# A hybrid diffusion layer on one core: the mLSTM's gate rows are multiplied third, and three merge-gate tiles move to other stages

## The reference

```python
p = split_in(h @ w_in)      # h: modulated RMSNorm of x; pc likewise for the context
y_a = mlstm_branch(q, k, v, o, gates)     # bidirectional, chunkwise
y_b = mla_branch(...)                     # latent attention
y_c = natten_branch(...)                  # neighbourhood attention
g_a, g_b, g_c = jnp.split(jax.nn.sigmoid(gate_pre), 3, axis=-1)   # the merge gates
y = (g_a * y_a + g_b * y_b + g_c * y_c) @ w_out
x = x + g1 * y
x = x + g2 * sqrelu_mlp(rms_norm(x, g_norm2) * (1 + sc2) + sh2, w_ff1, w_ff2)
```

## Time and profile before

| | us |
|---|---|
| median of 3 runs | 1851.31 (1850.52 to 1851.66) |
| the profiled execution: its time | 1852.28 |
| its span | 1850.6 |
| PE busy | 1663.7 |
| DVE, ACT, POOL busy | 972.6, 781.6, 668.1 |

### The profile page before, as it was taken

How to read it: one execution, slowest core, us unless ns; L and a number is a source line. 1 busy time by engine, 2 the same in 40 slices (tenths; PEclk the granted TensorE clock), 3 DMA queues, 4 the chain that set the end, 5 groups by cost and what they waited for, 6 DMA issues and landing times.

```text
span 1850.6 us, 24651 instructions
## 1 busy us (share of the span) xinstructions
PE 1663.7 (90%) x9536; PEld 1397.9 (76%) x9536; DVE 972.6 (53%) x1751; ACT 781.6 (42%) x1484; POOL 668.1 (36%) x389
## 2 busy tenths in 40 slices
PE   6998989899878988899999998978999788689998
PEld 3876779767666667688888886977977676589998
DVE  5855817662334545349496964143244264546665
ACT  4334734343645432432323234347434564245443
POOL 0632434412233001445454553524633342124443
PEclk9998999999989999999999999989999898889999
DMA  8432443401214113224354743322421232335553
GB/s 334 187 135 103 156 134 146 148 23 36 86 53 137 29 55 133 92 93 177 140 182 168 281 165 114 100 85 89 149 69 51 90 106 68 141 115 173 185 184 120
DMA packets 68059, 232.72 MB, mean 126 GB/s; under 512 B 18280, under 2 KB 22760, under 8 KB 54376
## 3 DMA queue, kind: packets, MB, share of 16 engines
q1 hardware_dynamic: 60880, 213.67, 32.9%
q10 hardware_dynamic: 7064, 17.49, 2.5%
...
## 4 chain that ended last, share of the span: by engine, by line
PE 70%; DVE 10%; ACT 10%; issue 4%; POOL 3%; DMA 2%; DVEq 0%; SPq 0%; ACTq 0%
PE bank L1683 33%; PE bank L1765 8%; PE bank L1721 7%; PE bank L1703 4%; PE bank L2033 4%; PE bank L2012 3%; PE bank L1747 2%; PE bank L2019 2%; ACT wH L770 2%; POOL wL L657 1%; DMA raw<-in_p_out 1%; DVE acc L1164 1%; PE bank L1914 1%; DVE mjunk L1161 1%; POOL wL L659 1%
## 5 line engine op out<-in xcount | busy, mean ns | idle before, releaser
L657 POOL TENSOR_TENSOR wL<-raw,wH 128x1280 fp32r<-128x1280 f32 (+4 forms) x146 | 307.4, 2105 | 610.7 <-ACT wH L770 610.7
L770 ACT ACTIVATE wH<-raw 128x768 fp32r<-128x768 f32 (+7 forms) x396 | 296.7, 806 | 538.5 <-PE bank L1683 353.2
L659 POOL TENSOR_TENSOR wL<-raw,wH 128x768 fp32r<-128x768 f32 (+3 forms) x198 | 322.3, 1628 | 392.9 <-ACT wH L770 392.8
L1683 PE MATMUL bank<-hH,wH 128*128 128x512 f32 (+1 forms) x704 | 241.7, 343 | 4.6 <-DVE oL L1556 2.9
L1683 PE MATMUL bank<-hL,wH 128*128 128x512 f32 (+1 forms) x704 | 239.6, 340 | 0.0
L1683 PE MATMUL bank<-hH,wL 128*128 128x512 f32 (+1 forms) x704 | 239.6, 340 | 0.0
L1683 PE MATMUL bank<-oH,wH 128*128 128x512 f32 (+1 forms) x576 | 196.8, 342 | 5.0 <-DVE wL L1146 5.0
L1683 PE MATMUL bank<-oL,wH 128*128 128x512 f32 (+1 forms) x576 | 195.6, 340 | 0.0
L1683 PE MATMUL bank<-oH,wL 128*128 128x512 f32 (+1 forms) x576 | 195.6, 340 | 0.0
L1164 DVE SCALAR_TENSOR_TENSOR acc<-acc,cb 128x1024 f32<-128x1024 f32 x88 | 170.9, 1955 | 2.5
L1721 PE MATMUL bank<-hH,wH 128*128 128x512 f32 (+1 forms) x384 | 141.6, 369 | 25.7 <-ACT gst L798 12.2
...
## 6 DMA issues: line engine op xcount, KB each, us to landing
raw<-in_p_ff SPq DMA_DIRECT2D x64, 1024.0 KB, 4.8
acc<-in_p_mod SPq DMA_DIRECT2D x44, 1024.0 KB, 5.6
raw<-in_p_ml SPq DMA_DIRECT2D x12, 1024.0 KB, 5.9
raw<-in_p_na SPq DMA_DIRECT2D x12, 1024.0 KB, 5.6
...
raw<-in_p_out SPq DMA_DIRECT2D x8, 1024.0 KB, 6.9
```

The source lines that it names most:

```text
L657: pool.tensor_tensor(l_[:, 0:cut], r_[:, 0:cut], h_[:, 0:cut].bitcast(F32), ALU.subtract)
L659: pool.tensor_tensor(l_[:, cut:k * w], r_[:, cut:k * w], h_[:, cut:k * w].bitcast(F32), ALU.subtract)\
L770: act.activation(flat(wH, n)[:, part], flat(raw, n)[:, part], ACT.Copy)\
L1683: ins = pe.matmul(dst, w_[:, kk, c:c + P], r_[:, kk, lo:TOK], start=kk == k0 and m == 0, stop=kk == k0 + kn - 1 and m == 2)
```

## The change

The gate-row block becomes key ("ml", l, 2), behind q and k; the values are 3 and 4, the output gate 5 and 6. On PE the small transposes stand between the two halves of block 3 and behind it, the transposes to columns (now to bank 5) between blocks 5 and 6. DVE does its part of the gate rows between the values' copies, and `mod(5)` to `mod(7)` move behind parts of it. ACT's exp and ln move up behind block 3. The part "chain" is gone: "last" has 4 tiles in place of 3, "cn" 5 and 6 in place of 3 and 4. `TURN` becomes branch 0, then 2, then 1. SP's modulation loads move to other places between the weight loads. Layer 0's tile 19 is loaded ahead of the key-value block. The blocks of two kinds, "wo" and "ff", may only be placed at multiples of their size.

Cut: renumbered lists in `gate_range`, `gate_bank` and `gates`, where the name "chain" goes.

```diff
--- before.py
+++ after.py
@@ -144,13 +144,13 @@
 MOD_START, MOD_PROJ, MOD_LOOP, MOD_ML = 4, 8, 14, 20
-LOOP_MODS = (3, 4, 8, 9, 10, 11, 12, 13)
+LOOP_MODS = (1, 2, 5, 6, 7, 8, 9, 10)
...
 GATES = 24
-TURN = [(2, c) for c in range(6)] + [(0, c) for c in range(KC)] + [(2, 6), (2, 7)] + [(1, c) for c in range(KC)]
-FILL = (dict(chain=3, loop=8, last=3, cn=3, units=(0, 2, 0, 1, 1, 1, 1, 1)),
-        dict(chain=3, loop=8, last=3, cn=4, units=(1, 1, 1, 1, 1, 1)))
+TURN = [(branch, c) for branch in (0, 2, 1) for c in range(KC)]
+FILL = (dict(loop=8, last=4, cn=5, units=(0, 2, 0, 1, 1, 1, 1, 1)),
+        dict(loop=8, last=4, cn=6, units=(1, 1, 1, 1, 1, 1)))
@@ -200,13 +200,11 @@
         both(("dq", l, 0), ("dq", l, 1), ("dk", l, 0), *(g[T] for T in gate_range(l, "cn")))
-        at = gate_range(l, 0).start
-        if l == 0:
-            load += [("uq", l, 0), g[at], g[at + 1], ("uq", l, 1), ("ukv", l, 0), *g[at + 2:]]
-            use += [("uq", l, 0), g[at], g[at + 1], ("uq", l, 1), *g[at + 2:at + 6], ("ukv", l, 0), *g[at + 6:]]
-        else:
-            load += [("uq", l, 0), g[at], ("uq", l, 1), g[at + 1], ("ukv", l, 0), *g[at + 2:]]
-            use += [("uq", l, 0), g[at], ("uq", l, 1), *g[at + 1:at + 5], ("ukv", l, 0), *g[at + 5:]]
+        stages = [("uq", l, k // 2 if l == 0 else k) for k in range(4 if l == 0 else 2)] + [("ukv", l, 0)] * 4
+        for k, key in enumerate(stages):
+            fill = [g[T] for T in gate_range(l, k)]
+            load += ([key] if stages.index(key) == k else []) + fill
+            use += ([key] if key not in stages[k + 1:] else []) + fill
         both(*(("ms", l, c) for c in range(KC)), *(("to", l, j) for j in range(4)),
@@ -429,7 +427,7 @@
             if name == "ml":
-                return (packed("p_ml", l, j), KC, BLK) if j < 6 else (packed("p_gk", l, 0), KC, 64)
+                return (packed("p_gk", l, 0), KC, 64) if j == 2 else (packed("p_ml", l, j - (j > 2)), KC, BLK)
             if name == "ff":
@@ -446,7 +444,7 @@
                 return max(RANK[m] if m >= 0 else -1 for m in held[at:at + size])
-            at_ = min(range(QUARTERS - size + 1), key=lambda at: (last_use(at), at))
+            at_ = min(range(0, QUARTERS - size + 1, size if KEYS[n][0] in ("wo", "ff") else 1), key=lambda at: (last_use(at), at))
             place.append(at_ * QUARTER)
@@ -589,8 +585,8 @@
                 load("ml", 0, j)
-                if MOD_START + j - 2 < MOD_PROJ:
-                    load_mod(MOD_START + j - 2)
+                if j != 5:
+                    load_mod(MOD_START + j - 2 - (j == 6))
             for l in range(DEPTH):
@@ -861,24 +857,24 @@
                 u0 = U0["ml", l]
+                tag = f"ml{l}_"
                 act.wait_ge(*S("spilled").at(16 * (l + 1)))
...
                             act.activation(m_k[:, b, :], full(u0 + j, b)[:, :], ACT.Copy).then_inc(free(u0 + j, b), 1)
-                        if j in (4, 5):
-                            act.activation(m_o[:, 2 * (j - 4) + b, t0:], full(u0 + j, b)[:, t0:TOK], ACT.Sigmoid)\
+                        if j in (5, 6):
+                            act.activation(m_o[:, 2 * (j - 5) + b, t0:], full(u0 + j, b)[:, t0:TOK], ACT.Sigmoid)\
                                 .then_inc(free(u0 + j, b), 1)
-                tag = f"ml{l}_"
-
-                exp_and_ln()
-                for d in range(2):
-                    act.wait_ge(*S(tag + "nz").at(d + 1))
-                    link(act.activation(m_e[d][0:4, :], m_e[d][0:4, :], ACT.Exp))
-                for d in range(2):
-                    act.activation(m_e[d][0:4, :], m_e[d][0:4, :], ACT.Ln, bias=1.0).then_inc(S(tag + "ln").up(1), 1)
-                gates_out(l, "chain")
+                    if j == 3:
+                        exp_and_ln()
+                        for d in range(2):
+                            act.wait_ge(*S(tag + "nz").at(d + 1))
+                            link(act.activation(m_e[d][0:4, :], m_e[d][0:4, :], ACT.Exp))
+                        for d in range(2):
+                            act.activation(m_e[d][0:4, :], m_e[d][0:4, :], ACT.Ln, bias=1.0)\
+                                .then_inc(S(tag + "ln").up(1), 1)
@@ -1247,26 +1243,28 @@
                     mod(MOD_START)
-                    mod(MOD_START + 1)
-                for j in (2, 3):
-                    for b in range(2):
-                        free(dve.tensor_copy(m_v[:, 2 * b:2 * b + 2, 2 * j - 4:2 * j - 2, 0:ML_DV],
-                                             full(u0 + j, b)[:, :].rearrange("p (t h w) -> p t h w", t=2, h=2)), u0 + j, b)
-                    if l == 0:
-                        mod(MOD_START + j)
+
+                def values_out(j, b):
+
+                    free(dve.tensor_copy(m_v[:, 2 * b:2 * b + 2, 2 * j - 6:2 * j - 4, 0:ML_DV],
+                                         full(u0 + j, b)[:, :].rearrange("p (t h w) -> p t h w", t=2, h=2)), u0 + j, b)
...
                 narrow = m_tmp[0:64, :]
-                free(dve.tensor_copy(narrow, full(u0 + 6, 0)[0:64, :]), u0 + 6, 0)
-                freed(u0 + 6, 0)
-                free(dve.tensor_tensor(narrow, narrow, full(u0 + 6, 1)[0:64, :], ALU.add), u0 + 6, 1)
+                free(dve.tensor_copy(narrow, full(u0 + 2, 0)[0:64, :]), u0 + 2, 0)
+                freed(u0 + 2, 0)
+                free(dve.tensor_tensor(narrow, narrow, full(u0 + 2, 1)[0:64, :], ALU.add), u0 + 2, 1)
                 dve.wait_ge(*S(tag + "turned").at(1))
...
                     .then_inc(S(tag + "small").up(1), 1)
+                values_out(3, 0)
                 for d in range(2):
...
                     dve.scalar_tensor_tensor(e, z, -1.0, z, ALU.mult, ALU.min).then_inc(S(tag + "nz").up(1), 1)
+                values_out(3, 1)
+                if l == 0:
+                    mod(MOD_START + 1)
                 for d in range(2):
@@ -1291,8 +1289,13 @@
                     dve.wait_ge(*S(tag + "nmrow").at(k))
+                for b in range(2):
+                    values_out(4, b)
+                if l == 0:
+                    mod(MOD_START + 2)
+                    mod(MOD_START + 3)
                 dve.wait_ge(*S(tag + "gT").at(1))
-                dve.tensor_copy(stat[:, 128:192], bank[3][:, 0:64]).then_inc(S(tag + "gcol").up(1), 1)
+                dve.tensor_copy(stat[:, 128:192], bank[5][:, 0:64]).then_inc(S(tag + "gcol").up(1), 1)
                 k = S(tag + "gcol").n
@@ -1753,11 +1756,13 @@
-            def tokens(n, u, k, parts, sH, sL, at=None):
+            def tokens(n, u, k, parts, sH, sL, at=None, only=None):
...
                 for b, part in enumerate(parts):
+                    if only not in (None, b):
+                        continue
                     bk = begin(u, b)
@@ -1832,35 +1837,35 @@
                 first_units(n0, u0, both(KC, t0), both(KC, 0), hH, hL, lambda kk: low_ready(l, 0, kk))
-                tokens(n0 + 2, u0 + 2, KC, two, hH, hL)
-                tokens(n0 + 3, u0 + 3, KC, two, hH, hL)
-                features(n0 + 4, u0 + 4, KC, both(KC, t0), hH, hL)
-                features(n0 + 5, u0 + 5, KC, both(KC, t0), hH, hL)
-                H, L = weights(n0 + 6)
+                H, L = weights(n0 + 2)
                 for b in range(2):
-                    dst = begin(u0 + 6, b)[0:64, :]
+                    dst = begin(u0 + 2, b)[0:64, :]
                     for kk in range(4 * b, 4 * b + 4):
...
                                             start=kk == 4 * b and m == 0, stop=kk == 4 * b + 3 and m == 2)
-                    filled(ins, u0 + 6, b)
-                drained(u0 + 7)
+                    filled(ins, u0 + 2, b)
+                tokens(n0 + 3, u0 + 3, KC, two, hH, hL, only=0)
+                pe.wait_ge(*S(f"bank_free{2 * (u0 % 2) + 1}").at((u0 + 2) // 2 + 1))
                 for t in range(NTILE):
...
                 ins.then_inc(S(tag + "turned").up(1), 1)
+                tokens(n0 + 3, u0 + 3, KC, two, hH, hL, only=1)
                 pe.wait_ge(*S(tag + "small").at(1))
...
                     ins.then_inc(S(tag + "rows").up(1), 1)
-                gates(l, "chain")
+                tokens(n0 + 4, u0 + 4, KC, two, hH, hL)
+                features(n0 + 5, u0 + 5, KC, both(KC, t0), hH, hL)
                 for d in range(2):
...
                         at = (d * 4 + t) * 4
-                        pe.transpose(bank[3][:, at:at + 4], m_g[0:4, d, t * P:t * P + P], ident[0:4, 0:4])
-                        ins = pe.transpose(bank[3][:, 32 + at:36 + at], m_rows[0:4, 2 + d, t * P:t * P + P], ident[0:4, 0:4])
+                        pe.transpose(bank[5][:, at:at + 4], m_g[0:4, d, t * P:t * P + P], ident[0:4, 0:4])
+                        ins = pe.transpose(bank[5][:, 32 + at:36 + at], m_rows[0:4, 2 + d, t * P:t * P + P], ident[0:4, 0:4])
                 ins.then_inc(S(tag + "gT").up(1), 1)
+                features(n0 + 6, u0 + 6, KC, both(KC, t0), hH, hL)
                 pe.wait_ge(*S(tag + "gcol").at(1))
@@ -1891,7 +1896,7 @@
```

(4 more changed lines are left out.)

6 lines of the change are left out of this document (2 added, 4 removed).

## The result

The changed kernel takes 1868.82 us (median of 4 runs, 1868.0 to 1871.56). The ratio of its runs to those of the kernel before, estimated with its 95% interval, is 1.0103 (1.0085 to 1.012). The prediction was no change at 1851.5 us, with a range from 1843 to 1859: the change is slower, by 17.5 us against the 1851.31 of before. The profiled execution took 1868.0 us, its span is 1866.3 us, 15.7 more than before.

A forecast was written before the change was run, and what follows sets the result against it. PE, busy nine tenths of the span, bounds the kernel; time is won only where it idles or runs at half clock. Terms +1.2 - 1.2 + 0.4 - 1.1 + 0.9 = +0.2 us on 1852.3, so median 1851.5; range 1843 to 1859.

The forecast's parts named there:

- Part 9: Layer 0's weight loads: tile 3 lands just in time, from 38 us for DVE's list and 43.5 for PE.
- tile 3's weights come late: Slower rival, layer 0: modulations 5 to 7 lengthen beside POOL, delaying tile 3's load; 4 to 5 us lost, chance 0.16.
- Part 5: Loop's second broadcast: PE idle for ACT's chain, 4.5 us in layer 0, 2.5 in layer 1, plus clock 2.0 and 1.0.
- Part 3: Before block 4: PE waits for its split, 5.2 us in layer 0, 4.4 in layer 1, plus clock 2.0 and 1.5.
- Part 8: Inside the loop: small waits for tile splits go, but ACT's chain starts at the same place; 0, bound -1.5 us.
- Part 2: Before block 3: PE waits for its split, which the gate-row block mostly covers; 0.8 us left in each layer.
- Part 1: Three moved tiles in "last" and "cn": same price, waits of 5.7 and 3.2 us not filled; 0, bounds 0 and -8.
- Part 7: ACT elsewhere: +0.4 us at layer 0's first square, -1.1 in its second query stage, +0.9 in layer 1's "last".
- Part 4: Gate chain: blocks 4 and 5 hide DVE's rows, so 4.1 us go; the wait for a gate tile's low half goes too.

The follow-up runs named there:

- e_load: The changed kernel with SP's modulation loads 8 and 9 moved behind tiles 3 and 4, so tile 3 loads ahead of them: 1857.31 us.
- e_clock: The changed kernel with 22 extra products of 128x512, result unused, in PE's wait before block 4, both layers: 1861.63 us.
- e_tiles: The kernel before with only the move of the three gate tiles to "last" and "cn", the gate rows staying last: 1885.88 us.
- e_ring: The changed kernel with an 18th quarter in the ring, the gate-row block at the ring's end, and `mjunk` in bfloat16: 1851.71 us.

## Why the prediction was wrong

**Part 9, tile 3's DMA, is the step that failed first.** It said "just in time", with 5.5 us to spare, from 38 us for DVE and 43.5 for PE. PE's 43.5 was 44.2; DVE's 38 was 44.8. Term by term, predicted and measured: to the first results 4.6 and 7.8, modulation 5 at 10 and 9.0, the rows 10 and 13.1, the copies 1.4 and 1.2, modulations 6 and 7 at 12 and 13.8. So 6.3 of the 6.8 us lie in the gate rows' own operations, which were put at their price of before, when POOL was idle beside them. In the changed kernel they ran while POOL split: 3.19 us for an operation of 0.68, and 3.25 for a scan of 0.74. The prediction had the outcome as its rival "tile 3's weights come late", at 4 to 5 us, with a chance of 0.16. Measured is 9.24 - 4.5 = 4.7 against the forecast and 9.24 - 3.60 = 5.6 against e_load, which shows the cause. The path was the right one (SP's order, ACT at tile 3's split, the exponential behind it); what made DVE late was not: the rival had it from the modulation instructions, and these together took 0.7 us more than predicted. That its price came out right is in part luck.

**Part 5, the second broadcast's wait.** Layer 0, without tile 3: 4.5 predicted, 3.60 in e_load. Layer 1: 2.5 predicted, 4.57 measured. ACT's chain behind PE's end took the predicted time (6.8, measured 1225.45 to 1232.19). PE's work in it was put at 4.3 us from the kernel before, but those broadcasts and scores had run at 1.2 GHz; at 2.4 they take 2.3. The same slip made the old stretch look better than it was: its clock loss was counted for 2.3 us behind the wait and not for the 5.3 us of broadcasts and scores ahead of it, which take about 2.7 at 2.4 GHz. So of the 4.9 us by which this term and layer 1's clock were short, about 2.6 cancel. That the stretch came out at +0.9 for -1.2, and not further off, is luck.

**Parts 3 and 5, the clock.** The four falls were placed right. They were put at 2.0, 1.5, 2.0 and 1.0 us, in all 6.5, and each cost 2.4 to 3.0, in all 10.7, whether the wait ahead was 4.6 or 9.2 us long. e_clock shows the pair at block 4 as 2.6 and 2.4 us.

**Part 8 and the rest of the kernel.** "0" for stages that the change doesn't touch left out that the clock falls elsewhere when all is moved in time: +1.6 in layer 0's loop, about +3.3 in "cn", about +1.6 in layer 1's loop. This is 6.5 us for which the forecast had no term, and the upper bound of its range (1859) took in the late tile (1856) and 3 us beside it. Of the twelve kernels without added products in layer 0's "cn", four run its sums at 2.4 GHz in their traces (the kernel before, e_load, e_clock, e_tiles: 1.12 us each) and eight at 1.2 (2.07 us each from the second on). The latent projections ahead took 27.5 to 28.9 us in the four and 29.1 to 30.4 in the eight, so the clock differed before the sums began. What decides it was not settled: the stage starts at 468.80 us in the change and at 467.82 in e_clock.

**What held.** Part 3's wait before block 4 is 4.85 us in both layers for 5.2 and 4.4, and e_ring shows the ring as its cause. Part 2's is 0.72 for 0.8. Part 1: the wait of 5.7 us in "last" did not shrink with a tile more (5.71). The 3.2 us of "cn" are 1.89 in the change, where the tiles ahead ran at 1.2 GHz, and 3.2 again in e_load, where they ran at 2.4. Part 7: -1.4 for -1.1 in the query stage, and a wait 1.2 us longer in layer 1's "last" for +0.9. Part 4: the waits for DVE's rows and for the old gate tile went, though e_ring shows that the first was only covered by the wait ahead of it.

By the prediction's own terms: +0.2, and 4.7 for tile 3, 4.2 for the clock in the stretches, 2.1 for layer 1's broadcast, less the 2.6 that cancel, and 6.5 for the clock elsewhere, make 15.1; measured 15.7. The other differences are smaller than 1 us each and were not followed up. Experiments show the causes of the first two; the 6.5 us elsewhere are seen in the traces as the clock's, and why it fell there stays open.
